# Stick-breaking attention: each engine's part of a step shifted against the others, and a mask product left out

## The reference, cut to what matters

```
z = einsum('bqhd,bshd->bhqs', qb, k) * 64 ** -0.5
mask = kpos[None, :] < t[:, None]
log_1m = where(mask, log_sigmoid(-z), 0.0)
between = cumsum(log_1m, axis=3, reverse=True) - log_1m
w = where(mask, exp(log_sigmoid(z) + between), 0.0)
o = einsum('bhqs,bshd->bqhd', w, v)
```

## Time and profile before

| | us |
|---|---|
| median of 3 executions | 2881.71 (2880.14 to 2881.86) |
| the profiled execution, device time | 2887.82 |
| its span, first to last instruction | 2886.0 |
| PE matmuls busy | 2756.3 (96%) |
| PE weight loads busy | 2417.7 (84%) |
| DVE busy | 2001.6 (69%) |
| ACT busy | 1348.1 (47%) |
| POOL busy | 314.6 (11%) |
| mean granted TensorE clock | 0.977 of full speed |

### The profile page before, as it was taken

One profiled execution on the slowest core, in us unless ns is written; L12 is line 12 of the kernel. 1 busy time (PEld: TensorE's weight loads), 2 busy tenths in 40 slices (PEclk: granted clock), 3 DMA queues, 4 the chain that ended last, 5 costly groups with the idle time before them and its releaser, 6 DMA issues.

```text
span 2886.0 us, 43931 instructions
## 1 busy us (share of the span) xinstructions
PE 2756.3 (96%) x17298; PEld 2417.7 (84%) x17298; DVE 2001.6 (69%) x3889; ACT 1348.1 (47%) x2188; POOL 314.6 (11%) x178
## 2 busy tenths in 40 slices
PE   7999999999999999999999999999999899798997
PEld 7779999998888888899999988887866678676776
DVE  4676988975555655689889655556567768546588
ACT  3423544445454534335444445454334457343475
POOL 0004950000000001069200000000100000010000
PEclk9999999999999999999999999999899999999999
DMA  5343555455656652445454555565511469422586
GB/s 196 106 145 127 177 169 157 158 169 183 195 192 196 205 173 91 170 137 177 162 161 154 168 190 192 195 192 166 156 52 24 158 234 350 137 73 60 179 286 231
DMA packets 175261, 479.25 MB, mean 166 GB/s; under 512 B 27200, under 2 KB 43600, under 8 KB 175056
## 3 DMA queue, kind: packets, MB, share of 16 engines
q1 hardware_dynamic: 171808, 473.29, 50.0%
q10 hardware_dynamic: 3248, 3.15, 0.4%
HBM read 474.80 MB, written 1.57 MB: 165 GB/s over the span
## 4 chain that ended last, share of the span: by engine, by line
PE 86%; DVE 7%; ACT 3%; POOL 2%; issue 1%; DMA 0%; ACTq 0%; SPq 0%; DVEq 0%; POOLq 0%
PE ps L135 85%; POOL ring_rest L155 2%; PE ps L138 2%; DVE big L163 2%; DVE spl L155 1%; ACT big L141 1%; DVE st L179 1%; ACT spl L141 1%; DVE big L155 1%; DVE xb L163 1%; ACT whi L141 0%; DVE st L163 0%; POOL big L155 0%; DVE xr L155 0%; DVE grouped L155 0%
## 5 line engine op out<-in xcount | busy, mean ns | idle before, releaser
L141 ACT ACTIVATE whi<-ring 128x1024 fp32r<-128x1024 f32 x512 | 543.0, 1061 | 686.7 <-PE ps L135 686.5
L135 PE MATMUL ps<-xr,whi 128*128 128x256 f32 x4096 | 749.8, 285 | 11.1 <-POOL ring_rest L155 10.7
L155 DVE TENSOR_TENSOR ring_rest<-ring,whi 128x1024 fp32r<-128x1024 f32 x412 | 503.6, 1223 | 319.5 <-ACT whi L141 319.5
L135 PEld LDWEIGHTS ps<-xr,whi 128*128 128x128 f32 x4096 | 639.6, 192 | 14.0 <-DVE big L185 8.6
L135 PE MATMUL ps<-whi,Ar 128*128 128x512 f32 x2048 | 632.1, 390 | 4.5 <-DVE Ar L155 4.5
L135 PE MATMUL ps<-xr,ring_rest 128*128 128x256 f32 x2048 | 580.4, 283 | 0.0
L155 DVE TENSOR_TENSOR spl<-ring,spl 128x1024 fp32r<-128x1024 f32 (+3 forms) x384 | 435.6, 1164 | 162.5 <-ACT spl L141 153.5
L135 PEld LDWEIGHTS ps<-whi,Ar 128*128 128x128 f32 x2048 | 385.1, 188 | 84.7 <-DVE Ar L155 5.0
L141 ACT ACTIVATE spl<-ring 128x1024 fp32r<-128x1024 f32 (+3 forms) x384 | 373.7, 1008 | 96.7 <-PE ps L135 76.8
L135 PE MATMUL ps<-ring_rest,Ar 128*128 128x512 f32 x1024 | 398.9, 390 | 0.0
L135 PEld LDWEIGHTS ps<-xr,ring_rest 128*128 128x128 f32 x2048 | 393.8, 192 | 0.0
(11 more groups left out here) (127 smaller groups left out, 2545.9 us busy)
## 6 DMA issues: line engine op xcount, KB each, us to landing
ring<-in_peer_u_dram SPq DMA_DIRECT2D x256, 512.0 KB, 3.5
ring<-in_peer_v_dram SPq DMA_DIRECT2D x256, 512.0 KB, 3.5
ring<-in_moe_gate_up_dram SPq DMA_DIRECT2D x128, 512.0 KB, 5.2
ring<-in_moe_w_down_dram SPq DMA_DIRECT2D x64, 512.0 KB, 5.2
ring<-in_peer_w_q_dram SPq DMA_DIRECT2D x32, 512.0 KB, 5.0
ring<-in_sb_w_in_dram SPq DMA_DIRECT2D x24, 512.0 KB, 4.4
ring<-in_ab_w_in_dram SPq DMA_DIRECT2D x20, 512.0 KB, 5.4
ring<-in_w_out_dram SPq DMA_DIRECT2D x16, 512.0 KB, 4.5
```

The lines of the kernel that those rows point to most:

```text
L135: return self.e.matmul(o, l, r, start=start, stop=stop)
L141: return self.e.activation(o, i, f, **k)
L155: return self.e.tensor_tensor(o, a, b, op)
```

## The change

In step s PE now does 6 for head s-3 and 1 for head s; DVE does 4 for head s-2, 7 for head s-3, and 2 for head s; ACT does 8 for head s-4 and 3 for head s-1. So everything that ACT reads was written by DVE in step s-1 or earlier, and what DVE and PE read of ACT's and DVE's is likewise one step older. The product with the mask (5) is taken out, with its constant `sbmul` and the DMA that brought it; a masked z is -1e30, for which the softplus is 0 already. Two more steps stand in the finish (18 and 19), and rows 3 and the transposes are placed one half-unit later.

```diff
-LATE = ("dil0", "dil1", "causal1", "sbmul", "sbadd", "scan", "glamask", "slots")
+LATE = ("dil0", "dil1", "causal1", "sbadd", "scan", "glamask", "slots")
...
-        sbmul, sbadd = scr[:, 13824:14208], scr[:, 14208:14592]
+        sbadd = scr[:, 13824:14208]
...
         def stick_step_pe(pe, s):
-            h = s - 2
+            h = s - 3
             if 0 <= h < 16:
                 b, e = 6 + h % 2, sbe[h % 4]
                 pv = bank(b)
                 take(pe, b)
-                pe.wait_ge(*gps.at(("sbs", h)))
                 pe.wait_ge(*vec.at(("sbp", h)))
...
         def stick_step_dve(dve, s):
-            h = s - 1
+            h = s - 2
             if 0 <= h < 16:
                 e = sbe[h % 4]
                 dve.wait_ge(*acted.at(("sbl", h)))
...
-            h = s - 2
+            h = s - 3
             if 0 <= h < 16:
                 dve.wait_ge(*psum.at(("sbc", h)))
...
         def stick_step_act(act, s):
-            h = s - 2
+            h = s - 4
             if 0 <= h < 16:
                 act.wait_ge(*vec.at(("sbw", h)))
                 act.activation(sbz[h], sbz[h], ACT.Exp).then_inc(*acted.next(("sbw", h)))
-            h = s
-            if h < 16:
+            h = s - 1
+            if 0 <= h < 16:
                 e = sbe[h % 4]
...
-        def stick_pool(pool):
...
-            late(act, "sbmul", sbmul)
...
                 stick_step(e, 17)
                 out_half(e, name, 0, 1, following)
+                stick_step(e, 18)
                 stick_rows(e, 2)
                 out_half(e, name, 1, 0, following)
-                stick_rows(e, 3)
+                stick_step(e, 19)
                 turn_rows(2)
                 out_half(e, name, 1, 1, following)
+                stick_rows(e, 3)
+                out_half(e, name, 2, 0, following)
                 turn_rows(3)
-                out_both(e, name, 2, following)
+                out_half(e, name, 2, 1, following)
                 out_both(e, name, 3, following)
```

More of the change, by code:

```diff
@@ L56, in constant_columns @@
     sb = np.concatenate([p < j, p < c], axis=1)
-    cols["sbmul"] = sb
     cols["sbadd"] = np.where(sb, 0.0, NEG)
@@ L2718, in gpsimd_program @@
             normed(pool, ("moe", 0), "x5m")
-            stick_pool(pool)
             mixed(pool, "wo3", "stick", "x5")
```

## The result

| | us |
|---|---|
| before, median of 4 (2880.14 to 2881.86) | 2881.34 |
| changed, median of 4 (2861.05 to 2864.90) | 2861.97 |
| ratio, 95% interval | 0.9935 (0.9918 to 0.9952) |
| changed, the profiled execution | 2862.17, span 2860.2 |

By the medians the change made the kernel 19.4 us faster; by the ratio it is 18.7 us (0.65%). 2864.5 had been forecast, a gain of 17.2.

A forecast was written before the change was run, and what follows sets the result against it. PE was taken as the bound, busy 96% of the span, so only its stops and slow clock could be won: 5.03 + 4.18 + 3.89 + 3.68 + 0.44 = 17.2 us, from 2881.7 to 2864.5, range 2860 to 2872.

The forecast's parts named there:

- the loop: ACT and DVE wait for each other within each attention step, 5.28 us a round; shifted, PE's 4.79 sets the pace.
- A: PE's stop before `Sq1`: 0.65 of 4.11 us stays for ACT's copy of the last output; 3.46 won.
- its slow start: Slow matmuls on PE after a stop: 1.57 or 1.6 us won at each of the first three, 0 in the finish.
- B: PE's stop before `Sv0`: nothing stays of 2.58 us; with 1.6 of slow clock, 4.18 won.
- C: PE's stop before `Sv1`: 1.30 of 3.59 us stays for DVE's scaling and copy; 2.29 won, and 1.6 of clock.
- D: PE's stop in the finish, 6.99 us: 2.61 + 1.07 = 3.68 won from two DVE waits; 3.3 stays.
- first sum's wait: PE's 0.44 us wait before the first sum of a head, booked to the mask product; all won.
- The mask term: Taking the mask product off POOL wins 0.44 us at the first sum; its other 15 products win 0.
- the clock did not fall at A and C: Rival: the clock still falls at A and C, 1.6 us each; gain 14.0, time 2867.7; chance 0.14.
- The loop did not stay: Rival: the loop stays, A to C unchanged, only D and the mask won; 4.1 us, time 2877.6; chance 0.12.
- More than forecast: Rival: the stop of the finish falls under 2 us or keeps its clock; 1.6 to 3 us more, about 2862.4; chance 0.08.
- The last Exp: ACT's Exp ahead of rows 3 comes later; some 4 us cover it, so 0. Rival that it makes the kernel slower: chance 0.04.

The follow-up runs named there:

- `changed_again`: The changed kernel itself, run again as yardstick in a later series: 2868.27 us, ratio 0.9949 to the kernel before, stretch 114.28 us.
- `mask_back_again`: The changed kernel with the mask product put back on GpSimd, second try: 2864.13 us, ratio 0.9938 to the kernel before, stretch 114.30 us.
- `stop_back`: The changed kernel with ACT made late once by 13 useless copies, so the stop before `Sq1` returns: 2871.97 us, ratio 0.9960, stretch 121.54 us.
- `exp_same_step`: The changed kernel with only ACT's last Exp waiting for DVE within the same step: 2874.57 us, ratio 0.9971 to the kernel before, stretch 127.26 us.
- `exp_later_only`: The kernel before without the mask product, only ACT's last Exp reading from a step back: 2882.18 us, ratio 0.9997, stretch 133.45 us.
- `no_stops_2`: The changed kernel with PSUM banks taken later, DVE's copy and first output-projection unit earlier, first transposed quarter ahead of step 16: 2857.88 us, ratio 0.9907.
- `fill_stops`: The kernel before with useless matmuls in PE's four stops, and bank 7 taken at every projection part: 2883.80 us, ratio 1.0002, stretch 127.12 us.

## Why the prediction was right, step by step

The bound and the loop were read rightly. Either wait alone keeps the round of 5.2 to 5.3 us and, with it, most of the stops; with both gone, PE sets the pace at 4.80.

| term | forecast us | measured us |
|---|---|---|
| A, stop before `Sq1` | 4.11 to 0.65 | 4.11 to 0.68 |
| its slow start | 1.57 won | 0.94 + 0.67 = 1.61 won |
| B, stop before `Sv0` | 2.58 to 0 | 2.58 to 0 |
| its slow start | 1.6 won | (2.31 - 1.56) + (1.91 - 1.04) = 1.62 won |
| C, stop before `Sv1` | 3.59 to 1.30 | 3.59 to 1.25 |
| its slow start | 1.6 won | (2.30 - 1.64) + (1.91 - 1.04) = 1.53 won |
| D, stop in the finish | 6.99 to 3.3 | 6.99 to 3.19 |
| its slow start | 0 won | 4.66 - 2.98 = 1.68 won |
| first sum's wait | 0.44 won | 0.44 gone |
| sum | 17.2 | 19.0, of 19.46 in the stretch |

The stops left at A, C and D came within 0.03, 0.05 and 0.11 us. At D the two waits of DVE that were to go are gone. Timeline of DVE in the changed kernel, behind its last copy of the projection:

```profile
2578.44 0.68 DVE L151 COPY big<-ps 128x512 f32<-128x512 f32 x1
2579.04 2.35 DVE L154 TENSOR_TENSOR spl<-ring,spl 128x1024 fp32r<-128x1024 f32 x2
...
2582.24 1.28 DVE L154 TENSOR_TENSOR xr<-ps,xr 128x512 fp32r<-128x512 f32 x2
```

Neither the rest nor the splitting waits, where they had waited 2.53 and 1.07 us. The term that was off is the clock after D. I had let the stop of 3.3 us keep its slow start, since one of 2.58 had one. The changed kernel, `changed_again` and `mask_back_again` all had the stop of 3.19 and full speed behind it. That step reasoned from the length of a stop to the clock, and the length does not decide it (last section): `stop_back` had the same 3.19 and slow matmuls. So the rows at hand could not tell which of the two it would be.

The mask term was right by its number and wrong by its cause, which is luck. I booked 0.44 us to the product that was taken out. The shift alone wins them, and the product's removal wins nothing in either kernel: 114.30 against 114.28, and 133.95 against 133.74.

The rivals: the clock did not fall at A and C (1.66 and 1.64 us for the matmuls behind them, granted clock 1.00 in the windows of 2 us from 2514 to 2518 and from 2553 to 2557). The Trainium skill's "TensorE: Matmul & The Clock Gate", section "A second HAM failure mode: psum-queue depth-cycling", says that frequent small idle spells between groups of matmuls can make the clock go back and forth. Spells of 0.68 and 1.25 us did not lower it here, but two spells 39 us apart are not frequent ones, so this kernel does not test that. The row that I leaned on, full clock around a spell of 1.80 us, was weak support (last section). The loop did not stay.

"More than forecast", with a chance of 0.08, is the rival that came in, by its second condition: the stop of the finish kept its clock. It gave 2862.4, and 2861.97 was measured. That the main forecast of 2864.5 lies so near is in part luck too: outside the stretch the medians moved by 6 us from one series of runs to the next.

The last Exp was in time. Timelines of ACT and PE in the changed kernel, this Exp and rows 3:

```profile
2594.66 0.51 ACT L140 ACTIVATE big<-big 128x384 f32<-128x384 f32 x1
```

```profile
2599.07 2.79 PE L134 MATMUL ps<-big 128*128 128x64 f32 x24
```

It ended at 2595.2, 3.9 us ahead of rows 3, where 4 had been forecast, and PE did not wait.

What the time of the kernel outside the stretch does is not explained by the change: 6 us between the two profiled executions. The prediction put it down to the execution, and `changed_again` against the first profile of the same kernel shows 2.56 us of it (scores at 2501.42 and 2498.86).

## What to carry to other kernels

When two helper engines wait for each other by about the same total, draw the loop and count the waits within one step: here it opened only when the last of them was gone, and one half of the shift won next to nothing. Then look for the stops of the bounding engine at the ends of parts and not in the steps, price what stays of each from rows of its last copy, and add what the slow matmuls behind it cost. Taking out a short wait wins nothing while a later, larger one absorbs it.

## What the runs showed of the hardware that was not expected

The slow clock after a stop does not follow from the length of the stop. Windows of the granted clock (us, busy times, clock, DMA) just behind stops: first `exp_same_step`, after stops of 1.85 and of 2.97 us:

```profile
2535.00:2537.00 2.00, 1.58 (x6) 1.34 (x7) 0.43 (x1) 1.54 (x4) 0.00 (x0) 0.86 0.05 16
2537.00:2539.00 2.00, 2.00 (x8) 1.58 (x6) 1.27 (x2) 0.00 (x0) 0.00 (x0) 0.50 0.14 5
...
2560.00:2562.00 2.00, 2.00 (x13) 1.60 (x11) 1.77 (x3) 0.19 (x1) 0.00 (x0) 1.00 0.15 8
```

The shorter stop was followed by 0.50, that is 1.2 GHz, the longer by 1.00. Then the same stop of 3.19 us in `changed_again` and in `stop_back`:

```profile
2585.00:2587.00 2.00, 1.38 (x6) 1.20 (x7) 2.00 (x3) 1.49 (x3) 0.00 (x0) 1.00 0.92 178
```

```profile
2589.00:2591.00 2.00, 1.42 (x4) 1.16 (x5) 2.00 (x3) 1.45 (x3) 0.00 (x0) 0.53 0.94 176
```

Even the stop of 1.80 us behind the stretch, which the prediction took as safe, is not: it stands in all twelve traces, full speed followed in ten, and in `exp_later_only` and `no_stops_2` the clock fell (granted clock 0.50 in the windows 2646 to 2648 and 2617 to 2619). Timeline of PE in `no_stops_2`:

```profile
2614.78 0.66 PE L137 MATMUL ps<-cst,xb 128*128 128x128 f32 x4 [1.80 <-DVE xb L162]
...
2616.36 1.00 PE L137 MATMUL ps<-cst,xb 128*128 128x128 f32 x4 [0.50 <-DVE xb L162]
2617.02 1.63 PE L134 MATMUL ps<-xr,spl 128*20 128x256 f32 x6
```

Where it fell in the stretch, it cost between 1.4 us (last stop of `stop_back`) and 2.7 us (first stop of `stop_back`). A stop of 3 us is therefore worth 3 us, and either nothing more or 1.4 to 2.7; a forecast should carry both. What decides between them was not tried.

A second thing: with the clock full, the same schedule repeats in three traces to 0.02 us over 114 us, but the part of the program ahead of it, with the same matmuls, ended anywhere between 2498.0 and 2504.9 us (`fill_stops`, which adds waits there, left aside). A change of 2 us is seen in such a stretch of one trace and not in medians of a few runs.
